# Twelve memory projection steps moved into the self-attention, their weights rounded by GpSimd

## The reference, cut to what matters

```python
h = rms_norm(x, norm_mix_pre[l])
z, xbc, dt_raw, q, k, v = jnp.split(h @ w_in[l], split_at, axis=-1)
y_ssd = ssd_mixer(z, xbc, dt_raw, ...)
y_diff = diff_attention(q, k, v, cos, sin, lam, ...)   # softmax 0 - lam * softmax 1, causal, 4 heads
mixed = jnp.concatenate([y_ssd, y_diff], axis=-1) @ w_out[l]
x = x + rms_norm(mixed, norm_mix_post[l])
h = rms_norm(x, norm_mem_q[l])
mem_h = rms_norm(mem, norm_mem_kv[l])
c = cross_attention(h, mem_h, w_mq[l], w_mk[l], w_mv[l], w_mo[l])   # needs mem_h @ wk, mem_h @ wv
x = x + rms_norm(c, norm_mem_post[l])
h = rms_norm(x, norm_mlp_pre[l])
m = jnp.square(jax.nn.relu(h @ w_up[l])) @ w_down[l]
x = x + rms_norm(m, norm_mlp_post[l])
```

## Time and profile before

| | us |
|---|---|
| runs (3) | 1476.4 median, 1475.8 to 1477.04 |
| profiled execution, its span | 1475.4 |
| TensorE busy in it | 1443.8 (98%) |
| VectorE, ScalarE, GpSimd busy | 934.8, 685.1, 86.8 |
| input projection, last part (100 to 337) | 237, TensorE busy 236.1 |
| self-attention (337.4 to 451.7) | 114.3 |
| memory projection with the `mix` tiles (452 to 504) | 52, TensorE busy 52.0 |

### The profile page before, as it was taken

One profiled execution on the slowest core, in us unless ns is written; L12 is line 12 of the kernel. 1 busy time (PEld: TensorE's weight loads), 2 busy tenths in 40 slices (PEclk: granted clock), 3 DMA queues, 4 the chain that ended last, 5 costly groups with the idle time before them and its releaser, 6 DMA issues.

```text
span 1475.4 us, 21355 instructions
## 1 busy us (share of the span) xinstructions
PE 1443.8 (98%) x8008; PEld 1231.0 (83%) x8016; DVE 934.8 (63%) x1586; ACT 685.1 (46%) x1401; POOL 86.8 (6%) x132
## 2 busy tenths in 40 slices
PE   9999999999999999999999999999999999999998
PEld 7889999996669988888988787888888788888886
DVE  4873566737885524523623788887776575557898
ACT  6324222337885423523632565454454464454443
POOL 1000000000010001000000360000000000000011
PEclk9999999999999999999999999999999999999999
DMA  8211111112003621110012343664443697766463
GB/s 317 59 30 57 30 30 30 31 43 72 1 2 109 221 71 30 58 57 30 2 58 71 115 136 114 207 195 176 150 155 116 235 336 268 267 221 193 158 228 129
DMA packets 95381, 177.23 MB, mean 120 GB/s; under 512 B 9904, under 2 KB 34480, under 8 KB 93232
## 3 DMA queue, kind: packets, MB, share of 16 engines
q1 hardware_dynamic: 90384, 153.30, 30.6%
q10 hardware_dynamic: 4896, 22.58, 4.8%
HBM read 138.10 MB, written 37.75 MB: 119 GB/s over the span
## 4 chain that ended last, share of the span: by engine, by line
PE 66%; DVE 4%; issue 2%; ACT 2%; POOL 0%; POOLq 0%; DVEq 0%; ACTq 0%
PE ps L2083 20%; PE ps L2085 20%; PE ps L2084 20%; PE ps L2397 2%; PE ps L2139 1%; DVE nmax L1609 1%; DVE wq_l L1836 1%; ACT probs L986 0%; PE ps L2421 0%; PE ps L2315 0%; PE ps L2408 0%; PE ps L2277 0%; PE ps L2296 0%; ACT probs_t L1003 0%; DVE u_s L1883 0%
## 5 line engine op out<-in xcount | busy, mean ns | idle before, releaser
L2083 PE MATMUL ps<-wh,oph 128*128 128x256 f32 (+2 forms) x768 | 249.0, 324 | 0.0
L2084 PE MATMUL ps<-wl,oph 128*128 128x256 f32 (+2 forms) x768 | 244.9, 319 | 0.0
L2085 PE MATMUL ps<-wh,opl 128*128 128x256 f32 (+2 forms) x768 | 244.9, 319 | 0.0
L2083 PE MATMUL ps<-d_ring 128*128 128x512 f32 x448 | 175.1, 391 | 2.1 <-DVE d_ring L1957 2.1
L2085 PE MATMUL ps<-d_ring 128*128 128x512 f32 x448 | 175.1, 391 | 0.0
L2084 PE MATMUL ps<-d_ring 128*128 128x512 f32 x448 | 175.0, 391 | 0.0
L2085 PEld LDWEIGHTS ps<-wh,opl 128*128 128x128 f32 x768 | 145.1, 189 | 10.9
L2084 PEld LDWEIGHTS ps<-wl,oph 128*128 128x128 f32 x768 | 145.2, 189 | 10.5
L2083 PEld LDWEIGHTS ps<-wh,oph 128*128 128x128 f32 x768 | 145.0, 189 | 10.6 <-ACT vt L947 0.2
L752 POOL TENSOR_TENSOR rms<-stat,mhalf 128x1 f32<-128x1 f32 (+2 forms) x59 | 50.5, 860 | 1339.1 <-DVE stat L1338 1317.4
L1256 ACT ACTIVATE d_ring<-left_raw 128x512 fp32r<-128x512 f32 x112 | 70.4, 629 | 96.0 <-PE ps L2085 73.8
(11 more groups left out here) (354 smaller groups left out, 2948.5 us busy)
## 6 DMA issues: line engine op xcount, KB each, us to landing
right_raw<-in_w_down_dram SPq DMA_DIRECT2D x128, 256.0 KB, 3.9
u_kept_s<-us SPq DMA_DIRECT2D x64, 256.0 KB, 2.5
left_raw<-u_kept_s SPq DMA_DIRECT2D x64, 256.0 KB, 3.0
w_blk<-in_w_up_blocks_dram ACTq DMA_DIRECT2D x14, 1024.0 KB, 5.9
left_raw<-u_kept_a SPq DMA_DIRECT2D x48, 256.0 KB, 3.0
raw<-in_w_in_dram SPq DMA_DIRECT2D x16, 512.0 KB, 3.7
u_kept_a<-u SPq DMA_DIRECT2D x24, 256.0 KB, 2.4
x_in<-in_x_dram SPq DMA_DIRECT2D x8, 512.0 KB, 9.2
```

The source lines that it names most:

```text
L2083: te.matmul(o, lh, rh, start=first, stop=False)
L2084: te.matmul(o, lh, rl, start=False, stop=False)
L2085: return te.matmul(o, ll, rh, start=False, stop=last)
```

## The change

- Twelve of the sixteen memory steps (x = 0 to 11: all eight of the keys and four of the values) move into the self-attention, to the iterations n = 1, 2, 6, 10, 12, 16, 18, 22, 24, 28, 30 and 32 (`MEM_AT`). On TensorE each stands behind the scores of n and in front of the probabilities' transposes. It writes bank 7, the bank of P·V, so TensorE waits for P·V of n-4 to be read before it, and for its own result to be read (`mem_seen`) before P·V of n-3.
- ScalarE reads the result of such a step at the head of its iteration n.
- The rounding of the twelve weight halves that belong to these steps goes from ScalarE to GpSimd (`g.tensor_copy`). GpSimd does them between its powers, each as soon as the half is loaded and its slot free. VectorE makes the remainder at the end of its iteration n+1.
- Loading, squaring, normalising and transposing `mem` moves into the input projection (iterations 51 to 62 of that loop). The attention's first matmul waits for it. `KEEP` and the transposes at the attention's end go.
- The other four steps (x = 12 to 15) follow the attention, each with two tiles of `mix` behind it instead of one tile behind every second step.
- Buffers move: `kmt`, `m_in`, `h_mem`, `meml`, the junk outputs; four value steps go to `vm_first` and are copied to `vm` by a transfer.

```diff
-KEEP = 20
 def tr_bank(n):
-    return 2 * (n - TR_MEM) if TR_MEM <= n < TR_MIX else 4 + 2 * (n % 2)
+    return 4 + 2 * (n % 2)
+MEM_STEPS = 16
+MEM_AT = {n: x for x, n in enumerate((1, 2, 6, 10, 12, 16, 18, 22, 24, 28, 30, 32))}
...
# GpSimd
+            def mem_split(x):
+                for q in split_at(*STEPS[STEP0["mk"] + x]):
+                    pool.wait_ge(raw_loaded[q % 2], 16 * (q // 2))
+                    pool.wait_ge(w_hi, q)
+                    sem_of, n = unit_end(q // 2 - 2)
+                    pool.wait_ge(sem_of, n)
+                    slot, part, n = half_slot(q)
+                    g.tensor_copy(wh[:, slot, part], raw[:, q % 2, n]).then_inc(w_hi, 1)
+            def in_attention():
+                for n in range(len(ATT_STEPS) + 7):
+                    if n in MEM_AT:
+                        mem_split(MEM_AT[n])
+                    if n - 6 in O_COMPLETE:
+                        pow_step(("o", O_COMPLETE[n - 6]))
...
# ScalarE
+                if n == 51:
+                    act.wait_ge(ssd_b, NT)
+                    for i in range(MT):
+                        act.dma_start(m_in[:, i, :], ...).then_inc(x_loaded[i], 16)
...
+                if n == 54:
+                    for i in range(MT):
+                        act.wait_ge(x_loaded[i], 16 * 3)
+                        square(("mem", i), m_in[:, i, :], h_mem[:, i, :])
+                if n in (60, 61):
+                    tr_hi(TR_MEM + n - 60, memh[:, :, (n - 60) * P:(n - 59) * P])
...
             for n in range(NS + 3):
+                if n in MEM_AT:
+                    mem_evac(MEM_AT[n])
                 if n >= 2 and n - 2 < NS:
                     probs_evac(n - 2, 0)
...
-                if n in (6, 7):
-                    act.wait_ge(x_loaded[n - 6], 16 * 3)
-                    square(("mem", n - 6), m_in[:, n - 6, :], m_junk[:])
...
+            for x in range(len(MEM_AT), MEM_STEPS):
+                mem_split(x)
+                mem_evac(x)
+                for m in (2 * (x - len(MEM_AT)), 2 * (x - len(MEM_AT)) + 1):
+                    tr_hi(TR_MIX + m, ...)
...
# VectorE
+                if n == 57:
+                    dve.wait_ge(gain_b_loaded, 16)
+                    for i in range(MT):
+                        normalise(("mem", i), TR_MEM + i, m_in[:, i, :], gain_b[:], h_mem[:, i, :])
+                if n in (61, 62):
+                    tr_lo(TR_MEM + n - 61, memh[:, :, tok], meml[:, :, tok])
...
+                if n - 1 in MEM_AT:
+                    mem_split(MEM_AT[n - 1])
-                if n == 9:
-                    dve.wait_ge(gain_b_loaded, 16)
-                    for i in range(MT):
-                        normalise(("mem", i), TR_MEM + i, m_in[:, i, :], gain_b[:], h_mem[:, i, :])
...
# TensorE
+                if n in (59, 60):
+                    transpose_tile(TR_MEM + n - 59, lambda k: h_mem[:, n - 59, k * P:(k + 1) * P])
+            pe.wait_ge(lo_done, 2 * (TR_MEM + MT))
...
             for n in range(NS + 3):
-                if n == 2:
-                    for _ in range(KEEP):
-                        te.transpose(ps[:, 6, 0:P], ident[:], ident[:])
                 if n < NS:
                     scores(n)
+                if n in MEM_AT:
+                    if n >= 4:
+                        pe.wait_ge(o_ev, n - 3)
+                    mem_step(MEM_AT[n])
                 if 2 <= n < NS + 2:
                     probs_transpose(n - 2, 0)
                 if n >= 3:
...
+                    if n in MEM_AT:
+                        mem_seen(MEM_AT[n])
                     for b in range(i + 1):
                         ins = te.matmul(ps[:, 7, 0:P], probs_t[:, k % 2, b, :], vt[:, b, h * P:(h + 1) * P],
                                         start=b == 0, stop=b == i)
-                if n in (NS, NS + 1):
-                    mem_tile(n - NS)
-            pe.wait_ge(pt_ev, len(PT_PARTS))
-            pe.wait_ge(o_ev, NS)
...
+            for x in range(len(MEM_AT), MEM_STEPS):
+                mem_step(x)
+                if x == len(MEM_AT):
+                    pe.wait_ge(pt_ev, len(PT_PARTS))
+                    pe.wait_ge(o_ev, NS)
+                    pe.wait_ge(ev["mv"], VALUES_IN)
+                for m in (2 * (x - len(MEM_AT)), 2 * (x - len(MEM_AT)) + 1):
+                    transpose_tile(TR_MIX + m, lambda k: mix[:, k, i * P:(i + 1) * P])
```

More of the change, by code:

```diff
@@ L196 @@
 O_STEP = {i: n for n, i in O_COMPLETE.items()}
-POWS = ([("in", 0)] + [("y", i) for i in range(NT)] + [("mem", i) for i in range(MT)]
+POWS = ([("in", 0)] + [("mem", i) for i in range(MT)] + [("y", i) for i in range(NT)]
         + [("o", i) for i in MIX_TILES])
@@ L969, in _, with mem_evac, mem_split @@
                     act.wait_ge(gate_done, NT + i + 1)
-                    square(("y", i), mix[:, 0:4, i * P:(i + 1) * P], junk[:, 0:512].rearrange("p (k c) -> p k c", k=4))
+                    square(("y", i), mix[:, 0:4, i * P:(i + 1) * P], y_junk[:].rearrange("p (k c) -> p k c", k=4))
             steps = ATT_STEPS
             NS = len(steps)
-            def mem_hi(i):
-                tr_hi(TR_MEM + i, memh[:, :, i * P:(i + 1) * P])
+            def mem_evac(x):
+                name, st = STEPS[STEP0["mk"] + x]
+                g = STEP0["mk"] + x
+                act.wait_ge(pj_done, g + 1)
+                if x == 0:
+                    act.wait_ge(sq_done, SQ[("y", NT - 1)] + 1)
+                if name == "mk":
+                    dst = kmt[:, st, :]
+                else:
+                    half = vm_first if x in MEM_AT.values() else vm
+                    dst = half[:, st % MT, (st // MT) * UC:(st // MT + 1) * UC]
+                s.activation(dst, ps[:, bank(g), 0:UC], ACT.Copy).then_inc(ev[name], 1)
+            def mem_split(x):
+                for q in split_at(*STEPS[STEP0["mk"] + x]):
+                    split_hi(q)
             def attn_exp(n, c):
@@ L1592, in _ @@
                     ssd_last(SSD_LAST[n])
+                if n == 55:
+                    for i in range(MT):
+                        squares(("mem", i))
+                        mean(("mem", i), D)
+                if n == 57:
+                    dve.wait_ge(gain_b_loaded, 16)
+                    for i in range(MT):
+                        normalise(("mem", i), TR_MEM + i, m_in[:, i, :], gain_b[:], h_mem[:, i, :])
+                if n in (61, 62):
+                    tok = slice((n - 61) * P, (n - 60) * P)
+                    tr_lo(TR_MEM + n - 61, memh[:, :, tok], meml[:, :, tok])
                 if n >= Y_DONE + 2:
@@ L1643, in _ @@
                     y_mean(6 + n)
-                if n == NS + 2:
-                    for i in range(MT):
-                        tr_lo(TR_MEM + i, memh[:, :, i * P:(i + 1) * P], meml[:, :, i * P:(i + 1) * P])
-                if n == 8:
-                    for i in range(MT):
-                        squares(("mem", i))
-                        mean(("mem", i), D)
-                if n == 9:
-                    dve.wait_ge(gain_b_loaded, 16)
-                    for i in range(MT):
-                        normalise(("mem", i), TR_MEM + i, m_in[:, i, :], gain_b[:], h_mem[:, i, :])
+                if n - 1 in MEM_AT:
+                    mem_split(MEM_AT[n - 1])
                 if n - 7 in O_COMPLETE:
```

107 lines of the change are left out of this document (56 added, 51 removed).

## The result

The changed kernel takes 1482.36 us (median of 6 runs, 1480.24 to 1483.21), the one before 1476.61 (6 runs beside it, 1475.8 to 1477.5): ratio 1.0037, 95% interval 1.0026 to 1.0048. It is slower by 5.8 us; I had forecast 1478.3. The profiled execution took 1483.21 us, its span is 1481.5 (1475.4 before).

The account below looks back on a forecast made before the run. TensorE, 98% busy, was taken as the bound, with three engines sharing one attention loop with little slack. Terms summed to +1.9 us on the 1475.4 us span, 1477.3; with 1.0 for the runs' median, 1478.3 us, range 1471 to 1485.

Parts of the forecast that it names:

- the class that I gave the most chance: Measured time within 0.2% (3 us) of no change, 1473.4 to 1479.4 us; chance 0.40.
- the likeliest case: The forecast's summed terms hold, 1478.3 us, with its own range of 1474.5 to 1481.5; chance 0.50.
- The weights of a new unit: In the attention, TensorE waits for VectorE's remainder before x = 4, 6, 8 and 10: +5.9 us.
- Rival 1: Waits overlap in the attention: VectorE reaches its remainder while TensorE is busy, giving 1472.3 us; chance 0.20.
- The step after a run: Where no memory step follows, VectorE's remainder delays a maximum ScalarE awaits, after n = 6, 12, 18, 24: +2.0 us.
- GpSimd: GpSimd's casts in the attention hold VectorE instructions with two SBUF inputs: +0.3 us, ends 0 and 13 us.
- The start: Attention's start: memory steps x = 0 and 1 at n = 1 and 2 take the place of idle transposes: -3.0 us.
- Transposes: Input stage: 16 transposes of the memory rows go where TensorE is full: +1.9 us.
- a memory step in the middle: Nine steps, n = 6 to 30, each delay the next scores 0.1 us beyond their 2.88 us: +1.0 us with rounding.
- the end: Attention's end: x = 11 fills waits and x = 12 starts at once after the last P·V: -3.7 us.
- rival 3: The clock falls after waits and memory steps run at 1.2 GHz; two hit give 1484.1 us; chance 0.08.
- rival 2: GpSimd casts hold the comb (VectorE's subtraction of the two softmaxes): six caught 1484.6 us, all twelve 1491; chance 0.15.

Follow-up runs that it names:

- experiment 1: Changed kernel with VectorE's remainder (second half of a weight split) one iteration earlier, beside its memory step, from n = 6 on: 1473.04 us, ratio 0.9978 to before.
- experiment 2: Changed kernel with the memory steps at n = 1, 2, 6, 8, 12, 14, 18, 20, 24, 26, 30, 32: 1477.53 us.
- experiment 3: Changed kernel with only the four remainders made for x = 3, 5, 7 and 9 one iteration earlier: 1477.89 us, ratio 1.0006 to before.
- experiment 7: Changed kernel with remainders one iteration earlier from n = 6 on and ScalarE, not GpSimd, rounding at its iteration's head, before the copy: 1472.60 us.
- experiment 9: Changed kernel with GpSimd's cast for x = 5 moved in front of the two powers of n = 13 and 14: 1482.24 us.
- experiment 5: Changed kernel with ScalarE instead of GpSimd rounding the twelve weight halves, at its iteration's end behind the exponentials: 1482.84 us.
- experiment 10: Kernel before with only the memory rows moved into the input projection; all sixteen memory steps follow the attention, idle transposes kept: 1475.81 us.
- experiment 8: Changed kernel with each of GpSimd's twelve casts done twice, one after the other: 1485.47 us, ratio 1.006 to before.

## Why the prediction was partly right

**The sign and the size.** 1482.4 lies in the range, but outside the class that I gave the most chance and the likeliest case's own range. The predicted span sum was +1.9; it is +6.1.

**The weights of a new unit: right.** Predicted 1.4 to 1.65 us before x = 4, 6, 8 and 10, +5.9 in all; measured 1.00 to 1.46, 4.9 in all, and the four stretches are 5.6 us shorter without them (experiment 1). They are shown to be VectorE's order by experiments 1, 2 and 3. Rival 1, overlapping waits, is excluded.

**The step after a run: right in kind, too small.** +2.0 predicted as half of the remainder's 1.22 us. Experiment 1 gives 3.0 back there, 1.1 of it at n = 14, where I had 0.5. That pair has a normalising of 0.68 us (`mix`) between the remainder and the comb; I had walked a generic pair and not that one. What makes the remainder dearer there is not shown: the normalising alone is not it, since with remainder and cast away (experiment 7) the pair costs 0.2 us.

**GpSimd: too small at one place.** I had 0.3 us by the casts' moments. The cast of x = 5, queued behind a power, caught the ratio in front of a comb for which TensorE waited: 0.8 us (experiment 9); with the 0.2 at n = 5 (experiments 5 and 7) GpSimd cost 1.0. One reading behind the term was wrong: in the earlier trace rows the two operations do not end together, GpSimd's ends at 860.65 and VectorE's at 861.20. As a rival for the whole loss GpSimd is excluded by experiment 5, and its upper end of 13 us with it.

**The start: too much gained.** -3.0 predicted, -1.9 measured. Of the missing 1.1 us 0.8 stand at the later `ACT_TABLE_LOAD` and come with the memory rows, not with the memory steps (experiment 10), and 0.2 the remainder held at n = 5. The sum had no term for the first: I had taken ScalarE's and VectorE's share of the memory rows at nothing, and had not followed what ScalarE does at the attention's first exponential.

**The rest.** Transposes +2.1 for +1.9; a memory step in the middle costs nothing beyond its 2.88 us (n = 16 to 18, 22 to 24 and 28 to 30 sum to 0.0); the end with x = 12 at once after the last P·V -3.7 for -3.7; four steps with two tiles of `mix` each hide all else, as worked out.

**The clock.** I gave a fall 8% and named the attention. It fell elsewhere, in the MLP behind a wait that both kernels have, in the profiled execution of the changed kernel and of experiment 1, not of experiment 5. It is 1.6 us of the 6.1 between the two profiled spans. It is not the medians' 5.8 us: at the same mean clock the changed kernel is 5.3, 5.5 and 5.7 us above before (table above). That a fall follows a wait and not always (0.62 in experiment 3, 1.00 in the changed kernel behind the same 1.69 us) is shown; what decides it is not. The sum had no price for it beyond rival 3, and it hides gains as well as losses: 2 of the 4.9 us that part experiment 3 from experiment 1, and more than half of experiment 8's 3.1.

**What the change could have been.** With the remainder one iteration earlier it takes 1473.0 us, and with ScalarE's rounding at the head of the iteration (experiment 7) 1472.6, the lowest of those tried. The time came out 4.1 us above the forecast. The mechanism that was to decide it held; what failed are sizes of the sum: the start 1.1 us too well, for the most part a term put at nothing, the step after a run 1.0, GpSimd 0.7, and in the profiled execution the clock 1.6. The units' waits erred the other way, by 0.3 (by the starts) to 1.0 us (by the waits). That 1482.4 lies inside the range owes something to its width: its upper end was drawn for rivals 2 and 3, and neither came true as written (one comb held late, a fall in another place).

## What to carry to other kernels

When work is woven into a loop of several in-order queues, each engine's part has its own right place: where that engine already waits for the longest piece of the new work. Here the same remainder cost 9 us one iteration later, and the same rounding 15 us behind the exponentials instead of in front of the copy. Walk the queue at every distinct place, not for a typical pair, before moving work to a third engine. And compare executions of one mean clock where a term is smaller than what a clock fall costs: here a rise of 0.001 in the mean went with 0.9 to 2.0 us less in the same kernel.

## What the runs showed of the hardware

A VectorE operation of one element per partition with SBUF operands took 0.99 instead of 0.22 us, to the end of a GpSimd cast of 1.04 us (the changed kernel and experiment 9): its own size does not limit what such a meeting costs. What it costs followed what GpSimd's operation had left: with 0.99 us left the ratio took 0.77 more, with 0.38 left the remainder at n = 5 took 0.24 more, with 1.05 left experiment 8's comb 0.84 more, with 1.23 left the operation of the earlier trace rows 1.09 more. It goes the other way too. In experiment 1 a cast that meets a remainder takes 2.00 us, 0.9 of it after the remainder's end; GpSimd, and VectorE at the same time:

```profile
387.81 2.00 POOL L793 CAST wh<-raw 128x1024 fp32r<-128x1024 f32 x1 [23.23 <-PE ps L2143]
```

```profile
387.70 1.22 DVE L1385 TENSOR_TENSOR wl<-raw,wh 128x1024 fp32r<-128x1024 f32 x1
```

The Trainium skill, "GPSIMD Engine Reference", section 1 (Specifications), lets GpSimd contend with VectorE instructions of two SBUF inputs. The trace agrees (0.22 against 0.99 us), but of all such meetings only two cost time in the changed kernel, 0.8 and 0.2 us.

GpSimd's cast of 128x1024 from fp32 to fp32r takes 1.04 us undisturbed, about as long as ScalarE's 1.06.
